# Strassen pairs for 42 of the 48 input units of a gMLP layer, with the value tiles kept in DRAM

## The reference

```python
u, v, g = jnp.split(h @ w_in, 3, axis=-1)          # w_in is 1024 x 6144
u = jax.nn.gelu(u)
v = layer_norm(jax.nn.gelu(v), ln_g, ln_b)          # over the 2048 features
...
mixed = jnp.einsum('gts,bnsgc->bntgc', ws, vc) + b_s.T[None, None, :, :, None]
out = (u * mixed * jax.nn.silu(g)) @ w_out           # w_out is 2048 x 1024
```

## Time and profile before

| | |
|---|---|
| time of three runs | 2345.67, 2346.04, 2347.95 us; median 2346.04 |
| the profiled execution | its own time isn't listed apart from the three; its span lies 1.9 us under their median |
| span of the profiled execution | 2344.1 us, first to last instruction |
| busy in the span | PE 2307.9, PEld 2227.5, DVE 1227.9, ACT 898.1, POOL 127.8 us |
| chain that ended last | PE 44%, issue 44%, DVE 5%, POOL 3% of the span |

### The profile page before, as it was taken

One profiled execution on the slowest core, in us unless ns is written; L12 is line 12 of the kernel. 1 busy time (PEld: TensorE's weight loads), 2 busy tenths in 40 slices (PEclk: granted clock), 3 DMA queues, 4 the chain that ended last, 5 costly groups with the idle time before them and its releaser, 6 DMA issues.

```text
span 2344.1 us, 36097 instructions
## 1 busy us (share of the span) xinstructions
PE 2307.9 (98%) x15487; PEld 2227.5 (95%) x15487; DVE 1227.9 (52%) x1708; ACT 898.1 (38%) x1295; POOL 127.8 (5%) x109
## 2 busy tenths in 40 slices
PE   8999999999999999999999999999999999999997
PEld 7999999999999898887999999989999999999997
DVE  4444445445424747667367877275444544545135
ACT  6223323323322535556362475363224233233232
POOL 0000000000000004345000110000000000000000
PEclk9999999999999999999999999999999999999999
DMA  4111111111121351211322111331111111111213
GB/s 140 46 46 46 46 38 45 46 37 46 46 92 46 103 149 46 55 46 37 109 85 81 46 46 39 118 118 55 46 46 46 37 45 46 37 46 46 90 47 109
DMA packets 58654, 145.86 MB, mean 62 GB/s; under 512 B 8936, under 2 KB 29560, under 8 KB 58488
## 3 DMA queue, kind: packets, MB, share of 16 engines
q1 hardware_dynamic: 55088, 138.66, 18.4%
q10 hardware_dynamic: 3408, 4.90, 0.8%
HBM read 121.47 MB, written 18.37 MB: 60 GB/s over the span
## 4 chain that ended last, share of the span: by engine, by line
PE 44%; issue 44%; DVE 5%; POOL 3%; POOLq 2%; DVEq 2%; ACT 1%; DMA 0%; ACTq 0%; SPq 0%
PE ps L583 34%; PE ps L609 5%; POOL l_sc L558 3%; PE ps L669 2%; POOLq L557 1%; PE ps L751 1%; PE ps L896 1%; DVE l_hs L2090 1%; DVE w_lo L1482 0%; PE ps L744 0%; POOLq L555 0%; ACTq L1426 0%; DVE l_it L2087 0%; DVEq L2099 0%; DVE l_xc L2067 0%
## 5 line engine op out<-in xcount | busy, mean ns | idle before, releaser
L583 PE MATMUL ps<-l_h_hi,w_hi 128*128 128x344 f32 x2448 | 526.7, 323 | 3.1 <-DVE w_lo L1482 3.1
L583 PE MATMUL ps<-l_h_lo,w_hi 128*128 128x344 f32 x2448 | 519.8, 321 | 0.0
L583 PE MATMUL ps<-l_h_hi,w_lo 128*128 128x344 f32 x2448 | 516.3, 319 | 0.0
L583 PEld LDWEIGHTS ps<-l_h_hi,w_hi 128*128 128x128 f32 x2448 | 408.9, 188 | 7.5 <-DVE w_lo L1482 4.2
L583 PEld LDWEIGHTS ps<-l_h_lo,w_hi 128*128 128x128 f32 x2448 | 414.2, 189 | 0.0
L583 PEld LDWEIGHTS ps<-l_h_hi,w_lo 128*128 128x128 f32 x2448 | 407.8, 188 | 0.0
L1482 DVE TENSOR_TENSOR w_lo<-w_raw,w_hi 128x1024 fp32r<-128x1024 f32 x181 | 225.2, 1245 | 238.3 <-ACT w_hi L1029 228.1
L1645 DVE TENSOR_TENSOR l_tmp<-ps,rx 128x1032 f32<-128x1032 f32 x64 | 78.9, 1232 | 285.5 <-PE ps L583 285.4
L1029 ACT ACTIVATE w_hi<-w_raw 128x1024 fp32r<-128x1024 f32 x181 | 189.6, 1048 | 90.2 <-DMA w_raw<-in_wu 78.1
L583 PE MATMUL ps<-l_y_lo,w_hi 128*128 128x344 f32 x816 | 173.2, 320 | 0.0
L583 PE MATMUL ps<-l_y_hi,w_hi 128*128 128x344 f32 x726 | 154.8, 322 | 0.8 <-DVEq L2104 0.8
(11 more groups left out here) (260 smaller groups left out, 3623.9 us busy)
## 6 DMA issues: line engine op xcount, KB each, us to landing
w_raw<-in_wu SPq DMA_DIRECT2D x181, 512.0 KB, 3.5
x_save<-x SPq DMA_DIRECT2D x9, 1376.0 KB, 7.4
x<-x_save SPq DMA_DIRECT2D x21, 516.0 KB, 6.9
out_y<-x SPq DMA_DIRECT2D x5, 688.0 KB, 3.7
l_sw<-l_q SPq DMA_DIRECT2D x24, 129.0 KB, 3.5
x<-in_xt SPq DMA_DIRECT2D x4, 688.0 KB, 9.9
x<-in_xt SPq DMA_DIRECT2D x5, 516.0 KB, 7.0
x<-in_xt ACTq DMA_DIRECT2D x3, 516.0 KB, 3.6
```

What stands on the lines that cost most here:

```text
L583: mm = nc.tensor.matmul(ps[:, 3 * slot + ch, 0:CW], wt[:, w, k, :], mv[:, k, ch * CW:(ch + 1) * CW], start=(k == 0 and t == 0), stop=(k == ...
```

## The change

In both gMLP layers units 0 to 5 (v) stay as they are. The other 42 input units form 21 pairs: 5 of two v units, 16 of the u and g unit of one m. A pair is a 2 x 2 block product: two features blocks (the two units), two halves of the inputs (4 of the 8 steps k), two halves of the tokens (516 each). Strassen's scheme makes it of 7 block products with sums of blocks in place of 8. A block product is 4 steps k x 3 terms x 2 column chunks of 258 = 24 matmuls, a pair 168 matmuls of 258 columns in place of 144 of 344. Over both layers 2 x 21 x 168 = 7056 matmuls of 258 columns stand in the order of PE in place of 6048 of 344.

- Token sums (t1 to t4, two blocks each): ACT scales the 8 input tiles in place at the layer's start (`scale_tokens`), POOL makes 8 sums of 128x1032, ACT and DVE split them into high and low parts (`t_high`, `t_low`). PE's program puts products 0 to 6 of a pair in three pairs of PSUM banks (`PAIR_BANKS`).
- For each pair POOL makes 4 weight sums of 128x512, ACT 7 high parts and DVE 7 low parts of 128x512 (`operand_high`, `operand_lows`). Before, 2 units took 2 such steps of 128x1024 on each engine.
- For each pair ACT copies one product out (`copy_first`), DVE makes 6 combinations of PSUM with an SBUF tile (`combine` 0 to 5, 128x516), and POOL does the three scalings by `rx` that DVE's combinations leave over (`scale`). Before, DVE read out twice with 128x1032.
- Finished v tiles are stored to DRAM by SP and come back one at a time to two tiles `vstage` for `centred`, `normal`, `mixed` and `gated_mixed`; the product goes to DRAM too and comes back before the output units. Three ring buffers turn into the buffers for pairs while these last.
- `turn(m-1)` stands after product 2 of pair m, `mixing(m-1)` after product 4.

The diff, cut to its core:

```diff
+A_PLAIN = 6
+A_PAIRS = (3 * MA - A_PLAIN) // 2
+V_PAIRS = (MA - A_PLAIN) // 2
...
+        PAIR_BANKS = (0, 1, 0, 2, 1, 2, 1)
+        PAIR_STARTS = (True, True, False, True, True, False, False)
+        T_ORDER = (("t1", 0), ("t1", 1), ("t3", 0), ("t3", 1), ("t2", 0), ("t2", 1), ("t4", 0), ("t4", 1))
...
@@ gpsimd @@
+                def weight_sums(p):
...
+                    nc.gpsimd.tensor_tensor(L.wsums[w][:], two[:, 0:HT], two[:, HT:KT], ALU.add).then_inc(L.wsum.sem, 1)
+                    nc.gpsimd.drain()
+                    nc.gpsimd.tensor_tensor(L.wsums[w + 1][:], L.wsums[w][:], one[:, 0:HT], ALU.subtract).then_inc(L.wsum.sem, 1)
+                    nc.gpsimd.tensor_tensor(two[:, 0:HT], one[:, 0:HT], two[:, 0:HT], ALU.subtract).then_inc(L.wsum.sem, 1)
+                    nc.gpsimd.drain()
+                    nc.gpsimd.tensor_tensor(L.wsums[w + 2][:], one[:, HT:KT], L.wsums[w + 1][:], ALU.subtract).then_inc(L.wsum.sem, 1)
+                def scale(p, n, tile, cols):
+                    pool.wait_ge(*L.comb.at(6 * p + n + 1))
+                    nc.gpsimd.tensor_tensor(tile[:, cols], tile[:, cols], rx[:, cols], ALU.mult).then_inc(L.scaled.sem, 1)
+                for n in range(8):
+                    token_sum(n)
+                weight_sums(0)
+                for p in range(A_PAIRS):
+                    if p:
+                        scale(p - 1, 5, pair_tiles(L, p - 1)[0], SECOND)
+                    if p + 1 < A_PAIRS:
+                        weight_sums(p + 1)
+                    scale(p, 3, pair_tiles(L, p)[1], SECOND)
+                    scale(p, 4, pair_tiles(L, p)[1], FIRST)
+                scale(A_PAIRS - 1, 5, pair_tiles(L, A_PAIRS - 1)[0], SECOND)
...
@@ tensor @@
+                def pair_product(p, i):
+                    pe.wait_ge(*L.op_low.at(N_OPS * p + i + 1))
...
+                    bank_free(p, i)
+                    j, start, low = PAIR_BANKS[i], PAIR_STARTS[i], operand_low(L, N_OPS * p + i)
+                    for k in range(HT):
+                        for t in range(3):
+                            for ch in range(2):
+                                hi, lo = tokens(i, ch)
+                                mm = nc.tensor.matmul(ps[:, 2 * j + ch, 0:QW], low[:, k, :] if t == 2 else L.op_hi[i][:, k, :],
+                                                      lo[:, k, :] if t == 1 else hi[:, k, :],
+                                                      start=start and k == 0 and t == 0, stop=k == HT - 1 and t == 2,
+                                                      skip_group_check=not start)
+                    mm.then_inc(L.prod.sem, 1)
+                for p in range(A_PAIRS):
+                    m = p - V_PAIRS
+                    for i in range(N_OPS):
+                        pair_product(p, i)
+                        if m == 0 and i >= 4:
+                            layer_sums(i - 4)
+                        if m >= 1 and i == (4 if m == 1 else 2):
+                            turn(m - 1)
+                        if m >= 1 and i == (6 if m == 1 else 4):
+                            mixing(m - 1)
...
@@ scalar @@
+                    nc.scalar.activation(x[:, k, :], x[:, k, :], ACT.Copy, scale=g_pre[:, L.i, k:k + 1]).then_inc(L.t_scaled.sem, 1)
...
+                for k in (0, 1, 4, 5, 2, 3, 6, 7):
+                    scale_tokens(k)
+                gelu_plain(0)
+                gelu_plain(1)
+                t_high(0)
+                t_high(1)
+                gelu_plain(2)
+                for n in range(2, 6):
+                    t_high(n)
+                gelu_plain(3)
...
+                        if m == 1 and i == 0:
+                            read_sums(2)
+                            inverse_deviation()
+                        if m >= 1 and i == 0:
+                            silu(m - 1)
...
@@ vector @@
+                def operand_lows(s_):
+                    p, i = divmod(s_, N_OPS)
+                    dve.wait_ge(*L.op_high.at(s_ + 1))
+                    if i < 2:
...
+                    V.tensor_tensor(operand_low(L, s_)[:], operand_raw(L, s_)[:], L.op_hi[i][:], ALU.subtract).then_inc(L.op_low.sem, 1)
+                def combine(p, n):
+                    one, two = pair_tiles(L, p)
+                    dve.wait_ge(*L.prod.at(N_OPS * p + n + 2))
+                    partial = halves(L.partial[:])
+                    if n == 0:
+                        dve.wait_ge(*L.copied.at(p + 1))
+                        V.tensor_tensor(partial, banks(1), partial, ALU.add)
...
+                        V.tensor_tensor(halves(one[:, FIRST]), banks(0), halves(rx[:, FIRST]), ALU.mult)
+                    if n == 2:
+                        V.tensor_tensor(halves(two[:, SECOND]), banks(2), partial, ALU.add)
+                    if n == 3:
+                        V.tensor_tensor(halves(two[:, SECOND]), banks(1), halves(two[:, SECOND]), ALU.add)
+                    if n == 4:
+                        V.tensor_tensor(halves(two[:, FIRST]), banks(2), partial, ALU.add)
+                    if n == 5:
+                        V.tensor_tensor(halves(one[:, SECOND]), banks(1), partial, ALU.add)
+                    V.drain().then_inc(L.comb.sem, 1)
...
+                read_v(0)
+                read_v(1)
+                t_low(0)
+                t_low(1)
+                read_v(2)
+                for n in range(2, 6):
+                    t_low(n)
+                read_v(3)
...
+                        if i == 0 and p:
+                            combine(p - 1, 5)
+                        if m >= 1 and i == 3:
+                            gated(m - 1)
+                        if i >= 2:
+                            combine(p, i - 2)
+                        if N_OPS * p + i + 3 < N_OPS * A_PAIRS:
+                            operand_lows(N_OPS * p + i + 3)
...
+                        if m >= 2 and i == 0:
+                            centred(m - 1)
+                        if m >= 2 and i == 1:
+                            normal(m - 1)
+                        if m >= 2 and i == 5:
+                            mixed(m - 1)
+                        if m >= 2 and i == 6:
+                            gated_mixed(m - 1)
...
+                combine(A_PAIRS - 1, 5)
+                for m in range(4):
+                    low_part(m)
+                gated(MA - 1)
```

More of the change, by code:

```diff
@@ L53, in __init__, with take @@
         self.result = 0
-    def take(self, units, results):
-        at = self.unit, self.result
+        self.plain = 0
+    def take(self, units, results, plain):
+        at = self.unit, self.result, self.plain
         self.unit += units
         self.result += results
+        self.plain += plain
         return at
@@ L487, in _ @@
                 while u < L.u1:
+                    if L.kind == "a" and u == L.u0 + A_PLAIN:
+                        pairs(L)
+                        u = L.u0 + 3 * MA + 3
+                        continue
                     weights(u)
@@ L567, in _ @@
             LA, LB, LC, LZ = layers
+            pairs(LA)
             normals(LB)
@@ L570, in _ @@
                 gate_input(LC, m)
+            pairs(LZ)
         @block.tensor
@@ L795, in layer_a @@
+                mixing(MA - 1)
+                unit(ring(u + 3), 1, u + 3, r + 3, *first)
                 later_units(2, KT, u, r, *first)
@@ L1186, in gates, with copy_first @@
+                def copy_first(p):
+                    act.wait_ge(*L.prod.at(N_OPS * p + 1))
+                    if p:
+                        act.wait_ge(*L.comb.at(6 * p))
+                    else:
+                        act.wait_ge(*L.t_low.at(8))
+                    nc.scalar.activation(halves(L.partial[:]), banks(0), ACT.Copy).then_inc(L.copied.sem, 1)
                 def gates(m):
-                    act.wait_ge(*L.in_done.at(2 * m + (MA + 1)))
+                    act.wait_ge(*L.scaled.at(3 * (V_PAIRS + m) + 3))
@@ L1794, in layer_a @@
+                combine(A_PAIRS - 1, 5)
+                for m in range(4):
+                    low_part(m)
+                gated(MA - 1)
+                for m in range(4, KT):
+                    low_part(m)
+                centred(MA - 1)
                 normal(MA - 1)
                 out_low(0, 2)
-                mixed(MA - 1, 3)
+                mixed(MA - 1)
+                gated_mixed(MA - 1)
                 out_low(2, 5)
```

596 lines of the change are left out of this document (425 added, 171 removed).

## The result

| | before | after |
|---|---|---|
| median of the runs | 2346.08 us (2345.67 to 2347.95, 4 runs) | 2446.43 us (2446.03 to 2447.91, 4 runs) |
| ratio | | 1.0425, 95% interval 1.041 to 1.044 |
| span of the profiled execution | 2344.1 us | 2444.2 us |
| mean granted clock | 0.997 | 0.965 |

A forecast was written before the change was run, and what follows sets the result against it. PE was taken to bound the kernel by its number of matmuls and their pace. The terms -31 - 8 + 38 + 16 + 8 = +23 us gave a forecast of 2369 us, range 2285 to 2412.

The forecast's parts named there:

- Step 1: PE's matmuls of 258 columns start 122 ns apart; a pair takes 20.50 us, 2.23 less than before.
- Rivals B and E: 258-column matmuls: B, pace at the 113 ns floor, 2330 us, chance 0.06; E, 157.8 ns like 344 columns, 2530, chance 0.04.
- Step 2: The v pairs and first two bodies, where PE still paces: 14 pairs gain 2.23 us each, -31 us.
- Step 3: The 28 later bodies, with DVE taking turns with POOL: 25.0 us each against 25.34, -8 us.
- the ring: Later bodies: DVE from product 5 to the normalised tile, then PE to the next product 5; 13.4 + 11.4 + 0.2 us.
- Step 4: Start of each gMLP layer: 16 us stall before unit 4 plus 3 at the lower clock, +38 us for both.
- Step 5: Layer norm statistics: product 2 waits for a copy behind ACT's Ln and Exp, 8 us a layer, +16 us.
- rival A: Turns with POOL short or hidden, PE paces every pair: bodies of 23.1 us, 2291 us in all, chance 0.26.
- Step 6: End of the pairs: output unit 0 waits 4 us for the last combination and what follows, +8 us for both layers.
- DRAM at nothing: DRAM traffic of v and y, two transfers of 528 KB in a body, was taken to cost nothing.
- Rival D: POOL's operations take 1.6 us or DVE fills: bodies of 26.5 us, full start stalls, 2415 us, chance 0.14.

The follow-up runs named there:

- no_sums: The change with POOL's four weight sums of each pair left out, so it computes something else; 2304.24 us.
- late_sums: The change with one wait added: POOL's weight sums of the next pair start only after DVE's normalised tile; 2331.53 us, 0.9936 of the kernel before.
- filled: The change with 24 useless matmuls of 258 columns on PE where it pauses before `turn`; 2415.88 us, 30.6 less than the change.

## Why the prediction was wrong

- **Step 1, the matmul of 258 columns: right.** 120.4 ns against 122. Rivals B and E fall, and the change's own gain, 42 pairs x 2.5 us, is there: `no_sums` shows bodies of 22.83 (25.34 before) and v pairs of 20.24 (22.73).
- **Step 2, PE-paced pairs: near.** The v pairs came to 21.5 us in place of 20.5 from the third on, through turns with the weight sums (`no_sums`: gone). The step costed DVE's operations at their durations alone, 14 of 20.5 us, though step 3 had the turns in it. 2.7 us a layer.
- **Step 3, the ring: right in its mechanism, and the step that failed in its size.** It gave 13.4 + 11.4 + 0.2 = 25.0 us a body; measured were 14.4 + 12.9 = 27.4. `late_sums` shows that the turns with POOL are what makes PE wait. Of the missing 2.4 us, about 1.0 is the part on DVE, and 0.8 of that is the scale and offset: with one SBUF input it was costed at 0.82 and waits too (1.59), for a fourth weight sum where the step counted three. The other 1.5 us is the lower clock behind each pause of 3 us, a term that step 3 left at nothing: step 4 priced it for the start of a layer, step 3 didn't for a pause that comes back in every body. `filled` measured it by itself, 1.45 us. Over both layers the step is 55 of the 77 us between forecast and result: a gain of 8 was forecast, a loss of 47 measured.
- **Step 4, the layer's start: right in its sum, in part by luck.** +19.5 us for +19 up to pair 0, and the first gelu at 55.47 as worked out. But the pause is 18.07 us for 16, and the stretch at the lower clock behind it is some 11 matmuls, 1.4 us, for 25 and 3: two errors of opposite sign. The experiments on it add what the step didn't ask: the work was not late because of its place alone, and moving one piece made the next one late.
- **Step 5: right in size, half right in cause.** 7.21 us for 8, but a part of it was ACT's wait for a variance that DVE had made in turns with POOL; and the 3.0 us before the sums over features wasn't forecast. In bodies 0 and 1 that makes 4.4 us a layer over the forecast. The step's lower bound of 3.5 doesn't follow from its terms, 6.3 + 1.07 + 0.6 less one product of 2.93 being 5.0; the forecast used the upper value, rival A the lower.
- **Step 6: right,** 3.8 us for 4. The stretch at the lower clock behind it, 2.4 us a layer, wasn't counted, nor were the 2.2 us that come up in layers 1 and 2.
- **DRAM at nothing: right.** No wait of DVE for a v tile shows in the list of waits. Rival D (2415) had the direction and a body of 26.5, but from a POOL operation of 1.6 us or a full DVE: the operation has 1.26 to 1.30 by itself, and `no_sums` and `late_sums` show that DVE wasn't full. It too left out the clock, so that it comes nearest is luck.
- The range ended at 2412 since D's body was bounded by POOL's operation alone. Had step 3 carried the clock, 28 x 1.5 = 42 us more, the forecast would have been 2411; that is an estimate, as `filled` shows 30.6 us for the clock over both layers.

Which DVE operations wait for POOL is wider than the prediction had it: L2140 with 1.59 us for 0.82 and the COPY with 2.71 for 0.70 have one SBUF input each, while operations that read PSUM beside one SBUF tile stay at 0.70 (L2111 in `late_sums`). The Trainium skill (SBUF — State Buffer, "SBUF: two separate sides") describes the shared ports as an exclusive lock which an instruction holds for the whole of its run, and it takes in DVE operations in a two-port mode beside those with two SBUF inputs. By that, these rows agree with it if the scale and offset and the COPY run in such a mode, which no row shows. The Trainium skill (GPSIMD Engine Reference, "Key points"), on which the prediction drew, names both kinds; the prediction used only its half on two inputs.

## What to carry to other kernels

An operation that is moved to GpSimd is not off the path: find which VectorE steps between SBUF and SBUF run beside it, and put it where the longest chain of VectorE doesn't stand; one wait in the right place was worth 115 us here. A pause of TensorE that comes back in every round can cost itself and a slow stretch behind it (3.0 + 1.5 us in each of 24 bodies here; the 1.04 us pauses of the v pairs had no such stretch, their clock was 1.00), so look for both; where the stretch lies on a ring, it makes the ring longer and the next pause comes back. When one blocked step of a start is moved, list what the next waits for before running it, stores and buffer reuse too.
